# Two feed-forward projections of a two-block transformer kernel as 2x2 block products in seven multiplications

## What is computed

```python
def rms_norm(x, g):
    xf = x.astype(jnp.float32)
    y = xf * lax.rsqrt(jnp.mean(xf * xf, axis=-1, keepdims=True) + RMS_EPS)
    return (y * g.astype(jnp.float32)).astype(x.dtype)

def swiglu(x, wi, wo):
    gate, up = jnp.split(x @ wi, 2, axis=-1)
    return (jax.nn.silu(gate) * up) @ wo

def first_block(x, ...):
    h = x
    for li in range(DEPTH):          # 2
        h = h + 0.5 * swiglu(rms_norm(h, ffn1_norm[li]), ffn1_wi[li], ffn1_wo[li])
        ...                          # a mixer: gated linear attention, then sparse attention
        h = h + 0.5 * swiglu(rms_norm(h, ffn2_norm[li]), ffn2_wi[li], ffn2_wo[li])
    return rms_norm(h, final_norm)
```

## Time and profile before

| | us |
|---|---|
| median of 3 runs | 2772.16 (2771.46 to 2772.74) |
| profiled execution, its own time | 2773.5 |
| its span, first to last instruction | 2771.8 |
| PE busy in the span | 2718.9 |
| DVE / ACT / POOL busy | 1577.0 / 1205.8 / 624.0 |
| projections of the first layer, block 3 to the end | 39.6 to 262.7 |
| projections of the second layer | 552.8 to 793.0 |

### The profile page before, as it was taken

The page is one execution under the profiler, slowest core; times in us unless marked ns, Lnnn a source line. Parts: engine busy times, 40 slices in busy tenths (PEclk is TensorE's granted clock), DMA queues, the critical chain, the costliest instruction groups (busy, mean ns, idle before and its releaser), DMA issues.

```text
span 2771.8 us, 39060 instructions
## 1 busy us (share of the span) xinstructions
PE 2718.9 (98%) x14176; PEld 2210.0 (80%) x14176; DVE 1577.0 (57%) x2453; ACT 1205.8 (44%) x1814; POOL 624.0 (23%) x607
## 2 busy tenths in 40 slices
PE   8999999999999999999899999999999999899998
PEld 6888888788888888887778888877888888777777
DVE  5444336544443575435865764338777777676664
ACT  4333232443322333223553333236655555457775
POOL 3000013100001451003733530014322222123232
PEclk9999999999999999999999999999999999999999
DMA  5333332233333564333203653322222222122222
GB/s 151 93 97 93 99 83 77 84 91 98 98 92 98 144 185 134 93 97 84 84 12 110 189 159 95 99 74 77 69 69 69 69 69 69 43 74 64 68 61 69
DMA packets 484826, 255.23 MB, mean 92 GB/s; under 512 B 17843, under 2 KB 478422, under 8 KB 484710
## 3 DMA queue, kind: packets, MB, share of 16 engines
q1 hardware_dynamic: 484534, 253.40, 31.9%
q10 hardware_dynamic: 176, 0.27, 0.0%
HBM read 251.51 MB, written 2.13 MB: 92 GB/s over the span
## 4 chain that ended last, share of the span: by engine, by line
PE 91%; DVE 6%; ACT 1%; POOL 1%; issue 1%; DMA 0%; SPq 0%; DVEq 0%; POOLq 0%; ACTq 0%
PE bank L259 73%; PE bank L1881 2%; PE bank L1912 1%; PE bank L1914 1%; PE bank L1913 1%; DVE dsa_work L1578 1%; DVE w_lo L245 1%; DVE small L1572 1%; PE bank L1988 1%; PE bank L2796 1%; PE bank L2788 1%; PE bank L2025 1%; PE bank L2821 1%; DVE gdn_blocks L2385 1%; PE bank L981 1%
## 5 line engine op out<-in xcount | busy, mean ns | idle before, releaser
L259 PE MATMUL bank<-x_hi,w_hi 128*128 128x512 f32 x2320 | 936.6, 404 | 8.6 <-DVE w_lo L245 4.8
L259 PE MATMUL bank<-x_hi,w_lo 128*128 128x512 f32 x2320 | 907.6, 391 | 0.0
L259 PE MATMUL bank<-x_lo,w_hi 128*128 128x512 f32 x2320 | 906.7, 391 | 0.6 <-DVE x_lo L586 0.6
L245 DVE TENSOR_TENSOR w_lo<-w_raw,w_hi 128x1024 fp32r<-128x1024 f32 x429 | 531.0, 1239 | 556.3 <-ACT w_hi L239 555.7
L239 ACT ACTIVATE w_hi<-w_raw 128x1024 fp32r<-128x1024 f32 x429 | 450.6, 1055 | 621.4 <-PE bank L259 572.1
L259 PEld LDWEIGHTS bank<-x_hi,w_hi 128*128 128x128 f32 x2320 | 437.1, 188 | 106.5 <-issue 16.1
L259 PEld LDWEIGHTS bank<-x_hi,w_lo 128*128 128x128 f32 x2320 | 436.2, 188 | 93.2
L259 PEld LDWEIGHTS bank<-x_lo,w_hi 128*128 128x128 f32 x2320 | 437.5, 189 | 87.5 <-issue 3.6
L435 POOL TENSOR_TENSOR sumsq<-sumsq,sq 128x512 f32<-128x512 f32 x56 | 92.3, 1648 | 1293.0 <-ACT sq L421 1292.4
L259 PE MATMUL bank<-h_hi,w_hi 128*128 128x512 f32 x768 | 298.9, 389 | 1.6 <-DVE h_lo L1612 1.6
L259 PE MATMUL bank<-h_hi,w_lo 128*128 128x512 f32 x768 | 298.8, 389 | 0.0
(11 more groups left out here) (486 smaller groups left out, 3474.9 us busy)
## 6 DMA issues: line engine op xcount, KB each, us to landing
w_raw<-in_ffn_wi_dram SPq DMA_DIRECT2D x176, 512.0 KB, 3.8
w_raw<-in_ffn_wo_dram SPq DMA_DIRECT2D x64, 512.0 KB, 4.1
w_raw<-in_ada_w_dram SPq DMA_DIRECT2D x48, 512.0 KB, 4.9
w_raw<-in_a_w_in_dram SPq DMA_DIRECT2D x48, 512.0 KB, 4.0
w_raw<-in_b_w_in_dram SPq DMA_DIRECT2D x32, 512.0 KB, 4.2
...
```

The source lines that it names most:

```text
L245: dve.tensor_tensor(w_lo[s][:], w_raw[raw_of(b) % RAW][:], w_hi[s][:].bitcast(F32), ALU.subtract).then_inc(w_lo_done, 1)
L259: mm = pe.matmul(out, lhs[:, w], rhs(kt), start=first and kk == 0 and m == 0, stop=last and kk == len(kts) - 1 and m == 2)
```

## The change

In ffn0 and ffn1 (`SEVEN = (0, 1)`) ten pairs, number 4 to 13 of 22, are computed as a product of 2x2 blocks in seven multiplications in place of eight. The two rows of blocks are the gate tile and the up tile, split by halves of the 1024 inputs; the columns are the two halves of the tokens (256 each). A multiplication is a group of 4 subtiles x 3 passes = 12 matmuls of 256 columns (`seven_group`), seven groups make a pair.

- **Rows.** `x_part` is the residual times gain times `rstd` (8 DVE operations, four in each pair of the first turn), so the results need no scaling. POOL makes four sums and differences of its quarters (`parts_pool`, 1024 elements each), ACT and DVE split them into `t_hi`, `t_lo`, and split the quarters of `x_part` itself into `x_hi`, `x_lo` in place (`own_act`, `own_dve`), once the last plain block before is done. `rstd` is then set to ones for the 8 pairs behind.
- **Weights.** Per pair POOL makes four sums of halves of the two weight tiles (`both_pool`, `three_pool`, `low_pool`, `all_pool`, 512 elements each); ACT casts and DVE subtracts for five pieces (left, both and all of 512 elements, row and low of 1024) where it was two of 1024. The four weight slots are reused by group and not by block. SP loads wait for the sums that still read the buffer.
- **Results.** The gate and the up bank are put together from groups: some accumulate in the bank, ACT copies one quarter from bank to bank and one to `p7_copy`, DVE adds two of them. Silu reads the bank directly (`first_silu`, `last_silu`), 256 columns each, and the product takes its other operand from the bank too.
- The code of these pairs is written out and no loop; pairs 0 to 3 and 14 to 21 are as before.

PE waits in `last_pe` for `all_lo` and `last_joined` of the pair. The loop over DVE's steps stands in `seven_dve`, behind the entry that the second order below shows. On POOL `both_pool` waits, from the second pair on, for `both_lo` of the pair before, `three_pool` for `left_lo` of its own, and `all_pool` for `all_lo` of the pair before.

The core of the diff:

```diff
+SEVEN = (0, 1)
+SEVEN_AT, SEVEN_N = 4, 10
+HT = T // 2
...
                     dve.tensor_tensor(prod[s][:], prod[s][:], gate_s[s][:], ALU.mult).then_inc(prod_done, 1)
+                    if f in SEVEN and turn0 == 0:
+                        parts_dve(dve, f, gain, range(4 * s, 4 * s + 4))
...
+        def seven_group(pe, slot, h, x, out, first=False):
+            hi, lo = w_hi[slot], w_lo[slot]
+            x_h, x_l = x
+            for k in range(4):
+                w = slice(h * T + k * P, h * T + k * P + P)
+                for m, (lhs, rhs) in enumerate(((hi, x_h), (hi, x_l), (lo, x_h))):
+                    mm = pe.matmul(out, lhs[:, w], rhs[:, k, :], start=first and k == 0 and m == 0, ...)
...
+        def first_pe(pe, f, n):
+            c = seven(f) + n
+            if n >= 2:
+                pe.wait_ge(silu_done, seven_pair(f, n - 2))
+            if n == 0:
+                own_pe(pe, f, 0)
+            pe.wait_ge(left_lo, c + 1)
+            seven_group(pe, slot_of(f, 1), 1, own_pair(0, T1), seven_banks(f, n)[0][:, T1], n >= 2).then_inc(p1_done, 1)
+        def seventh_pe(pe, f, n):
+            ...
+            pe.wait_ge(both_lo, c + 1)
+            seven_group(pe, slot_of(f, 2), 0, part_pair(0), seven_banks(f, n)[0][:, T2], n < 2).then_inc(p7_done, 1)
...
+        def seven_pe(pe, f, one):
+            seventh_pe(pe, f, 0)
+            first_pe(pe, f, 0)
+            seventh_pe(pe, f, 1)
+            for n in range(SEVEN_N):
+                pe.wait_ge(row_lo, c + 1)
+                pe.wait_ge(p1_copied, c + 1)
+                ...
+                seven_group(pe, slot_of(f, 0), 0, part_pair(2), B[:, T1])
+                pe.wait_ge(p7_copied, c + 1)
+                ...
+                seven_group(pe, slot_of(f, 0), 1, own_pair(1, T1), A[:, T1]).then_inc(p2_done, 1)
+                if n:
+                    last_pe(pe, f, n - 1)
+                if n + 1 < SEVEN_N:
+                    first_pe(pe, f, n + 1)
+                    if n:
+                        seventh_pe(pe, f, n + 1)
+                pe.wait_ge(low_lo, c + 1)
+                pe.wait_ge(p7_joined, c + 1)
+                ...
+                seven_group(pe, slot_of(f, 3), 0, part_pair(1), B[:, T1])
+                seven_group(pe, slot_of(f, 3), 1, part_pair(3), B[:, T2]).then_inc(p4_done, 1)
...
+            for n in range(SEVEN_N):
+                if n:
+                    last_dve(dve, f, n - 1)
+                low_dve(dve, f, n)
+                if n and n + 1 < SEVEN_N:
+                    both_dve(dve, f, n + 1)
+                join_dve(dve, f, n)
+                if n < 2:
+                    own_dve(dve, f, 2 + n)
+                if n + 1 < SEVEN_N:
+                    row_dve(dve, f, n + 1)
+                ...
+                all_dve(dve, f, n)
+                if n:
+                    up_dve(dve, f, n - 1)
+                if n + 2 < SEVEN_N:
+                    left_dve(dve, f, n + 2)
+                if n:
+                    h_lo_dve(dve, f, n - 1)
...
+        def both_pool(pool, f, n):
+            pool.tensor_tensor(w_both[:], w_raw[raw % RAW][:, LEFT_H], w_raw[(raw + 1) % RAW][:, LEFT_H], ALU.add)...
+        def three_pool(pool, f, n):
+            pool.tensor_tensor(w_raw[raw % RAW][:, LEFT_H], w_both[:], w_raw[(raw + 1) % RAW][:, RIGHT_H], ALU.add)...
+        def low_pool(pool, f, n):
+            pool.tensor_tensor(w[:, LEFT_H], w[:, LEFT_H], w[:, RIGHT_H], ALU.add)...
+        def all_pool(pool, f, n):
+            pool.tensor_tensor(w_all[:], w[:, LEFT_H], w[:, RIGHT_H], ALU.add)...
```

More of the change, by code:

```diff
@@ L171, in first_and_second_block @@
         stage_rows = [tile(f"stage_rows{k}", 16 + k) for k in range(3)]
+        x_part, x_sum = tile("x_part", 4, KT), tile("x_sum", FT + 4, KT)
+        t_hi = [tile(f"t_hi{c}", FT + 14 + 2 * c, 2, F32R) for c in range(4)]
+        t_lo = [tile(f"t_lo{c}", 14 + 2 * c, 2, F32R) for c in range(4)]
+        w_both, w_all = tile("w_both", 13), tile("w_all", FT + 13)
+        p7_copy = [sumsq[:, 0:HT], sumsq[:, HT:T]]
         x_in = tile("x_in", 0, 8)
@@ L198, in first_and_second_block @@
         ada_made, ada_added, ada_summed = sem("ada_made"), sem("ada_added"), sem("ada_summed")
+        part_made, part_added, part_hi, part_lo = sem("part_made"), sem("part_added"), sem("part_hi"), sem("part_lo")
+        left_hi, both_hi, row_hi, low_hi, all_hi = (sem(f"{n}_hi") for n in ("left", "both", "row", "low", "all"))
+        left_lo, both_lo, row_lo, low_lo, all_lo = (sem(f"{n}_lo") for n in ("left", "both", "row", "low", "all"))
+        both_added, three_added, low_added, all_added = (sem(f"{n}_added") for n in ("both", "three", "low", "all"))
+        p1_done, p7_done, p2_done, p3_done, p4_done = (sem(f"p{n}_done") for n in (1, 7, 2, 3, 4))
+        p1_copied, p7_copied, p7_joined, last_joined = (
+            sem(n) for n in ("p1_copied", "p7_copied", "p7_joined", "last_joined"))
+        own_hi, own_lo, rstd_ones = sem("own_hi"), sem("own_lo"), sem("rstd_ones")
         normed = sem("normed")
@@ L686, in ffn_pe, with one @@
             b0, t0 = BASE[f"ffn{f}"]
-            if not ada_of(f):
+            if f in SEVEN:
+                def one(u, i=0, n=0, part=None):
+                    if not part:
+                        pe.wait_ge(tile_free, t0 + u + 1 + i * n)
+                    products(pe, b0 + u, bank[(t0 + u) % BANKS][:], x_of(x_hi), x_of(x_lo), range(KT), True, True, i, n, part)
+                project_pe(pe, run, b0, t0, 4, r, begun)
+                for u in range(4, 2 * SEVEN_AT):
+                    one(u)
+                seven_pe(pe, f, one)
+                o = 2 * (SEVEN_AT + SEVEN_N)
+                for u in range(1, 4):
+                    one(o + u)
+                with pe.Fori(1, (2 * FT - o) // 4) as i:
+                    for u in range(4):
+                        one(o + u, i, 4)
+            elif not ada_of(f):
                 project_pe(pe, run, b0, t0, 2 * FT, r, begun)
@@ L735, in ffn_act, with ffn_dve @@
             split_hi(act, b0 + AHEAD)
-            ffn_turns(act, f, turn)
+            if f in SEVEN:
+                for k in range(SEVEN_AT // 2 - 1):
+                    turn(4 * k, 4, k, 0, False)
+                seven_act(act, f)
+                k = (SEVEN_AT + SEVEN_N) // 2
+                with act.Fori(0, FT // 2 - k) as i:
+                    turn(4 * k, 4, k, i, False)
+            else:
+                ffn_turns(act, f, turn)
             down_act(act, b0 + 2 * FT, FT, after, 1)
-        def ffn_dve(dve, f, r, after, first=None):
+        def ffn_dve(dve, f, r, after, first=None, gain=None):
             b0, t0 = BASE[f"ffn{f}"]
@@ new lines, in slot_of, with seven_sp @@
+        def slot_of(f, k):
+            return (seven_block(f, 0) + k) % SPLIT
+        LEFT_H, RIGHT_H = slice(0, T), slice(T, 2 * T)
+        def seven_sp(sp, f, n, src):
+            raw = raw_of(seven_block(f, n))
+            c = seven(f) + n - 2
+            for m in range(2):
+                if n >= 2:
+                    if m == 0:
+                        sp.wait_ge(all_added, c + 1)
+                        sp.wait_ge(row_lo, c + 1)
+                    else:
+                        sp.wait_ge(low_lo, c + 1)
+                else:
+                    sp.wait_ge(w_lo_done, raw + m + 1)
+                dst = w_raw[(raw + m) % RAW].rearrange("p (k c) -> p k c", c=P)
+                sp.dma_start(dst, src(m)).then_inc(w_loaded[(raw + m) % RAW], 16)
@@ new lines, in own_pe @@
+        def own_pe(pe, f, m):
+            pe.wait_ge(own_lo, 4 * SEVEN.index(f) + m + 1)
+        def seven_group(pe, slot, h, x, out, first=False):
[4 more added lines that the diff above has]
+                for m, (lhs, rhs) in enumerate(((hi, x_h), (hi, x_l), (lo, x_h))):
+                    mm = pe.matmul(out, lhs[:, w], rhs[:, k, :], start=first and k == 0 and m == 0, stop=k == 3 and m == 2, skip_group_check=True)
+            return mm
@@ new lines, in row_dve, with low_dve @@
+        def row_dve(dve, f, n):
+            dve.wait_ge(row_hi, seven(f) + n + 1)
+            k = slot_of(f, 0)
+            dve.tensor_tensor(w_lo[k][:], w_raw[raw_of(seven_block(f, n)) % RAW][:], w_hi[k][:].bitcast(F32), ALU.subtract).then_inc(row_lo, 1)
+        def low_dve(dve, f, n):
+            dve.wait_ge(low_hi, seven(f) + n + 1)
+            k = slot_of(f, 3)
+            dve.tensor_tensor(w_lo[k][:], w_raw[(raw_of(seven_block(f, n)) + 1) % RAW][:], w_hi[k][:].bitcast(F32), ALU.subtract).then_inc(low_lo, 1)
@@ L3232, in _ @@
             start_pool(pool)
+            seven_pool(pool, 0)
             sums_pool(pool, 1)
@@ L3235, in _ @@
             sums_pool(pool, 2)
+            seven_pool(pool, 1)
             sums_pool(pool, 3)
```

341 lines of the change are left out of this document (338 added, 3 removed).

## The result

The median went from 2771.91 to 2788.67 us (2787.61 to 2789.19, four runs each side): ratio 1.0058, 95% interval 1.0044 to 1.0072, 16.8 us slower.

The account below looks back on a forecast made before the run. TensorE was taken as the bound, by columns streamed; -26.0 (pairs) + 23.3 (entries) + 9 (first and steady pairs) + 2 (clock) = +8.3 us, median 2780.5; the forecast's own range 2770 to 2790, the overall range 2756 to 2790.

Parts of the forecast that it names:

- PE, 20 pairs: TensorE in both layers: each changed pair takes 9.58 us in place of 10.88, so twenty pairs save 26.0 us.
- entries, with the clock: Where plain pairs give way to changed ones: PE idle 13.8 and 9.5 us, together 23.3, plus 2 for lowered clock.
- first and steady pairs: Changed pairs behind the entry: PE waits for DVE and POOL, 4.5 us a layer, 9 in two.
- The matmul's price: Changed pairs on PE: a matmul of 256 columns takes 0.114 us, half of 0.227 for 512.
- Rival (d): Weight load paces 256-column matmuls at 0.12 us or more, pair 10.1 or more: some +12, 2784; chance 0.60 shared with forecast.
- DVE and POOL exclude each other: Entries and changed pairs: a DVE operation on two SBUF tensors and a POOL operation wait for each other; alternating saves 0.13 to 0.15.
- Rival (a): DVE and POOL disturb each other far less; entry idle 3.2 and 7.5 us in total, -15.3, 2757 us; chance 0.20.
- The entry's chain: Second layer's entry, DVE and POOL taking turns: both_lo done at 600.9, own x_lo at 608.15; PE idle 9.5 us.
- The second wait: Second layer's entry: PE's second group waits for the own quarter's x_lo, 5.8 us.
- The clock: Behind the entries' idle stretches some 3.4 us of work runs at half clock: 1 us lost each, 2 in all, bounds 0 and 6.
- the ring of shared steps: Steady pairs: DVE's and POOL's alternating steps take 9.82 us, 0.24 above PE's 9.58, costing 1.3 us a layer.
- the first pairs: Pairs 1 to 3 behind each entry: both_lo and last_joined come late by 0.3 to 1.2 us, 3.2 a layer.

Follow-up runs that it names:

- the halves in the kernel before: Kernel before the change, with 528 projection matmuls of 512 columns each made as two of 256: 2779.1 against 2772.5 us.
- three fills: Changed kernel with each of POOL's sums replaced by three constant fills in a row that read nothing, results meaningless: 2773.2 us.
- eight pairs: Changed kernel with eight pairs (6 to 13) in place of ten, preparation spread over the six plain pairs ahead: 2774.4 us, ratio 1.0008.

## Why the prediction was right in direction and 8 us short

| term | predicted | measured |
|---|---|---|
| PE, 20 pairs | -26.0 | -16.0 (10.08 a pair) |
| entries, with the clock | 23.3 + 2 | 28.9 (16.4 and 12.4) |
| first and steady pairs | 9 | 2.1 |
| ahead of block 3 | 0 | -0.7 |
| behind the layers | 0 | 1.2 |
| sum | +8.3 | +15.5 |

An entry is counted up to the start of pair 1 (94.14 and 629.94), against block 8 of before, moved by what the trace was earlier or later until then (-0.7, +8.8), and eight groups of 1.44.

- **The matmul's price** is the step that failed, the term of 26.0. Its row had both values, 0.12 and 0.11, and I took the half of 0.227. Both were real: unrounded, 15 of the 16 such places have 113 or 114 ns for the first step and 119 or 120 for the second. I took the first, which belongs to two matmuls between other work; in a stream nearly every step is of the second kind, as the halves in the kernel before and the settled pairs both show. Over 1680 matmuls that is 10 us; the middle would have been 5 off. Rival (d) named this with its price of a pair, 10.1, and put the loss at some 12 us (its own terms give -16 + 23.3 + 2 = 9.3; where the rest comes from it doesn't say); I set it inside the forecast and let the centre stand at the other value. The Trainium skill ("TensorE: Matmul & The Clock Gate", Back-to-back issue gap) gives 109 ns for 256 columns; the measurement, 120, decides.
- **DVE and POOL exclude each other**: right, and the step that decided the sign. Without it (three fills) the kernel is at 2773. Rival (a) said 2757, which with the true pace is 2767; the rest is the groups at half clock, 2.4 us a layer, that it left out, and 1.0 us more of waiting.
- **The entry's chain**, followed step by step, was right to 0.2 us. both_lo was put at 600.9 and the own x_lo at 608.15; the layer starts 8.8 later, so 609.7 and 616.95, and the trace has 609.83 and 617.13. The idle before the first group, 3.7 and 8.0, came as 3.9 and 7.9. The second wait, put at 5.8, came as 4.3, since the group before it ran at half clock and filled 1.3 us of it.
- **The clock**: the granted clock fell as said, but for 17 us in the first layer, and not over some 3 us of work. In the table's row of entries the slow groups stand with 4.1 us a layer, 8.2 in all, against the 2 forecast, and the idle time with 20.4 against 23.3. What the clock cost in the end is another number: taken away, it gave back 1.0 us in each layer, which is the 2 us forecast. That DVE's lateness hides part was in the prediction; that it hides three quarters of 4.1, and not a part of 1.7, was luck.
- **Steady pairs**: with PE at 10.08, DVE's and POOL's 9.82 fit under it, so the ring of shared steps cost 0 and the first pairs 0.9 a layer, not 4.5 (0.1 more lies at the way out). Pair 2 to 3 took 10.99, all later ones 10.08. That this error of 7 hid part of the first one's 10 is luck: without it the median would lie above the range.

What stays open: the 1.2 us behind the layers. Over the traces this stretch varies from -1.1 to +1.2 with no order that I can see; with eight pairs the layers sum to +0.8 and the span is 1.6 shorter. Nor was it tested what sets block 3's beginning.
